# A mixture-of-experts stage on one Trainium2 core: 21 units of expert work instead of 22, two of them cut into strips of 64, 32 and 32 slots

## The reference, cut to what matters

```python
# h: 1024 tokens x 1024; N_GROUPS = 4, EXPERTS_PER_GROUP = 8, so 32 experts; EXPERT_FF = 512
gsel = argmax(h @ rg + rgb)                    # one group for each token
top_v, top_i = top_k((h @ re + reb)[gsel], 2)  # two experts in that group
wts = softmax(top_v) * p_group
# for each token and each of its two experts e:
y += wt * ((silu(h @ w1[e]) * (h @ w3[e])) @ w2[e])   # w1, w3: 1024x512, w2: 512x1024
x = rms_norm(x + y) * norm_final
```

## Time and profile before

| what | value |
| --- | --- |
| time, median of 3 runs | 2502.93 us (2500.17 to 2503.08) |
| profiled execution, its own time | 2497.98 us |
| span in its profile, first to last instruction | 2496.2 us |
| busy share of the span | PE 97%, PEld 52%, DVE 50%, ACT 23%, POOL 4% |
| mean granted clock of TensorE | 0.988 |
| HBM read, written | 329.07 MB, 68.26 MB |

### The profile page before, as it was taken

The page is one execution under the profiler, slowest core; times in us unless marked ns, Lnnn a source line. Parts: engine busy times, 40 slices in busy tenths (PEclk is TensorE's granted clock), DMA queues, the critical chain, the costliest instruction groups (busy, mean ns, idle before and its releaser), DMA issues. The chain is left out here.

```text
span 2496.2 us, 39012 instructions
## 1 busy us (share of the span) xinstructions
PE 2412.2 (97%) x16519; PEld 1288.4 (52%) x16519; DVE 1243.1 (50%) x2080; ACT 570.2 (23%) x949; POOL 99.8 (4%) x97
## 2 busy tenths in 40 slices
PE   9999999999999999989999999999999999999996
PEld 5644557454565454744445976644455444443342
DVE  4646676767675858563585634465444411101103
ACT  3322323223232424121111354411100000000002
POOL 1000000000000000000000000000000100000002
PEclk9999999999999999999999999999999999999998
DMA  4111212121212121122434823163263999999997
GB/s 155 40 49 38 70 49 70 45 70 49 70 45 64 38 79 35 61 65 73 161 76 127 302 97 102 39 208 109 74 220 133 413 428 428 427 427 424 428 428 294
DMA packets 214908, 406.18 MB, mean 163 GB/s; under 512 B 64979, under 2 KB 166861, under 8 KB 202445
## 3 DMA queue, kind: packets, MB, share of 16 engines
q1 hardware_dynamic: 187152, 336.42, 36.9%
q10 hardware_dynamic: 22108, 47.32, 5.2%
q0 software_dynamic: 5472, 19.93, 2.1%
HBM read 329.07 MB, written 68.26 MB: 159 GB/s over the span
## 5 line engine op out<-in xcount | busy, mean ns | idle before, releaser
L3317 PE MATMUL moe_pp<-moe_ring,own_xT 128*128 128x512 f32 (+1 forms) x624 | 235.5, 599 | 1.4 <-DVE own_xT L3072 1.4
L3175 DVE COPY own_hidT<-moe_pp 128x512 f32<-128x512 f32 x22 | 15.2, 691 | 270.9 <-PE moe_pp L3326 270.9
L3317 PEld LDWEIGHTS moe_pp<-moe_ring,own_xT 128*128 128x128 f32 (+1 forms) x624 | 89.7, 167 | 107.0 <-issue 105.0
L742 PE MATMUL rwkv_pp<-mix_hT,rwkv_side_raw 128*128 128x512 f32 x240 | 116.7, 621 | 8.0 <-DMA rwkv_side_raw<-w_in 4.1
L3340 PE MATMUL moe_pp<-moe_ring,own_hidT 128*64 128x512 f32 (+1 forms) x368 | 120.1, 594 | 0.8 <-DVE own_hidT L3175 0.8
L2881 PE MATMUL moe_pp<-moe_ring,mix_hT 128*128 128x512 f32 x256 | 117.5, 610 | 3.3 <-DVEq L179 3.3
L671 PE MATMUL rwkv_pp<-mix_hT,rwkv_wt_kv 128*128 128x512 f32 x256 | 113.3, 595 | 0.0
L742 PE MATMUL rwkv_pp<-rwkv_TS,rwkv_side_sum 128*128 128x512 f32 x240 | 109.9, 601 | 2.8 <-ACT rwkv_TT L1259 1.7
L742 PE MATMUL rwkv_pp<-rwkv_TS,rwkv_side_raw 128*128 128x512 f32 x240 | 110.6, 603 | 0.8
L1682 DVE TENSOR_TENSOR rwkv_Sf<-rwkv_pp,rwkv_LY 128x64 f32<-128x64 f32 x128 | 28.7, 225 | 161.0 <-PE rwkv_pp L1023 161.0
L2309 PE MATMUL attn_pp<-att_yC,attn_wp 128*128 128x512 f32 x224 | 100.7, 597 | 0.0
(11 more groups left out here) (493 smaller groups left out, 4459.3 us busy)
## 6 DMA issues: line engine op xcount, KB each, us to landing
moe_ring<-moe_w SPq DMA_DIRECT2D x54, 2048.0 KB, 31.6
mix_yAB<-moe_w SPq DMA_DIRECT2D x18, 2048.0 KB, 32.4
mix_hT<-moe_w SPq DMA_DIRECT2D x17, 2048.0 KB, 31.7
rwkv_side_raw<-w_in SPq DMA_DIRECT2D x20, 1024.0 KB, 5.4
s_y<-mix_yAB SPq DMA_DIRECT2D x24, 512.0 KB, 11.8
moe_ring<-moe_w ACTq DMA_DIRECT2D x6, 2048.0 KB, 9.0
s_y<-own_yo ACTq DMA_DIRECT2D x22, 512.0 KB, 10.4
rwkv_wt_kv<-w_in SPq DMA_DIRECT2D x16, 512.0 KB, 4.4
```

The lines of the kernel that those rows point to most:

```text
L742: mm = pe.matmul(pp[:, bank, :], left[:, part, :], right[:, part, :], start=fresh and part == 0, stop=part == HK - 1, skip_group_check=True)
L3175: dve.tensor_copy(hidT[:, :, :].rearrange("p k s -> p (k s)"), pp[:, 4, :]).then_inc(hidT_s, 1)
L3317: mm = pe.matmul(pp[at, bank, :], xT[n % 2][:, kt, at], weights(w, n, h)[0][:, kt, :], start=kt == 0, stop=kt == KT - 1)
```

## The change

The number of units falls from 22 to 21. The unit of rank 31 and rank 3's surplus is gone. Instead the two whole units with the fewest tokens, ranks 11 and 12 (`LENDERS = 2`), keep 96 slots and lend 32: rank 11 to the surplus of rank 3, rank 12 to rank 31. A function `columns` gives the strips of a unit for the matmuls: one of 128 in a whole unit, two of 64 in a shared one, and in the two lending units three: 64 and 32 columns with the lender's weights, 32 columns with the borrower's. The unit order changes from place 9 on: pairs of small experts are now two in a row at places 8 and 9, rank 3 and the unit (11, 3) stand at 10 and 11, and the list ends (29, 30), (12, 31), (10). The 96 weight loads stay 96, in the new order. `room` computes the new capacities and offsets, with 14 chained instructions on VectorE in place of 10. The ranges of the loops, the ring, the transfers of one unit and everything after the units are as before.

```diff
-WHOLE = 13
-SMALL = N_EXPERTS - WHOLE
-UNITS = WHOLE - STATIC_HALVES // 2 + (SMALL + 1) // 2
-TOP_HALF = 2 * UNITS - 1
+WHOLE = 13
+LAST = N_EXPERTS - 1
+HALVES = LAST - WHOLE
+LENDERS = 2
+UNITS = WHOLE - STATIC_HALVES // 2 + HALVES // 2
...
+    wholes = [((r,), r - shared) for r in range(TOP + 1, WHOLE - LENDERS)]
+    pairs = [((WHOLE + 2 * j, WHOLE + 2 * j + 1), WHOLE - shared + j) for j in range(HALVES // 2)]
+    pairs.append(((WHOLE - 1, LAST), WHOLE - 1 - shared))
+    top = [((TOP,), TOP - shared), ((WHOLE - 2, TOP), WHOLE - 2 - shared)]
...
+    middle = len(wholes) // 2
+    return first + mixed(pairs[:middle + 2], wholes[:middle]) + top + mixed(pairs[middle + 2:-1], wholes[middle:-1]) + [pairs[-1], wholes[-1]]
+
+def columns(ranks):
+    if len(ranks) == 1:
+        return [(0, slice(0, SLOTS))]
+    if WHOLE - LENDERS <= ranks[0] < WHOLE:
+        cut = SLOTS - QUARTER_SLOTS
+        return [(0, slice(0, HALF_SLOTS)), (0, slice(HALF_SLOTS, cut)), (1, slice(cut, SLOTS))]
+    return [(0, slice(0, HALF_SLOTS)), (1, slice(HALF_SLOTS, SLOTS))]
...
             def room():
                 link(dve.scalar_tensor_tensor(out=base[:, :], in0=rank[:, :], scalar=float(WHOLE), in1=rank[:, :], op0=ALU.min, op1=ALU.add))
-                link(dve.tensor_scalar(cap[:, :], rank[:, :], float(WHOLE), float(HALF_SLOTS), ALU.is_lt, ALU.mult))
-                link(dve.scalar_tensor_tensor(out=cap[:, :], in0=rank[:, :], scalar=float(STATIC_HALVES), in1=cap[:, :], op0=ALU.is_ge, op1=ALU.mult))
+                link(dve.tensor_scalar(cap[:, :], rank[:, :], float(STATIC_HALVES), -2.0, ALU.is_ge, ALU.mult))
+                for r in (WHOLE - LENDERS, WHOLE, LAST):
+                    link(dve.scalar_tensor_tensor(out=cap[:, :], in0=rank[:, :], scalar=float(r), in1=cap[:, :], op0=ALU.is_ge, op1=ALU.add))
...
             def up(w, bank, done, n):
                 landed(pe, w, n)
-                many = len(RANKS[n])
-                rows = P // many
                 for kt in range(KT):
-                    for h in range(many):
-                        at = slice(h * rows, h * rows + rows)
+                    for h, at in columns(RANKS[n]):
                         mm = pe.matmul(pp[at, bank, :], xT[n % 2][:, kt, at], weights(w, n, h)[0][:, kt, :],
                                        start=kt == 0, stop=kt == KT - 1)
                 mm.then_inc(done, 1)
```

More of the change, by code:

```diff
@@ L61 @@
 HALF_SLOTS = SLOTS // 2
+QUARTER_SLOTS = SLOTS // 4
 STATIC_EXPERTS = (0, 2, 1)
@@ L81, in unit_order, with mixed, lent @@
 def unit_order():
-    assert SMALL // 2 == WHOLE - TOP - 1
+    assert HALVES % 2 == 0
     shared = STATIC_HALVES // 2
[L86 to L92, removed]
-    first = [(tuple(range(STATIC_HALVES)), 0)] + [((r,), r - shared) for r in range(STATIC_HALVES, STATIC)]
-    return first + mixed(slice(0, middle)) + top + mixed(slice(middle, None))
+    wholes = [((r,), r - shared) for r in range(TOP + 1, WHOLE - LENDERS)]
+    pairs = [((WHOLE + 2 * j, WHOLE + 2 * j + 1), WHOLE - shared + j) for j in range(HALVES // 2)]
+    pairs.append(((WHOLE - 1, LAST), WHOLE - 1 - shared))
+    top = [((TOP,), TOP - shared), ((WHOLE - 2, TOP), WHOLE - 2 - shared)]
+    first = [(tuple(range(STATIC_HALVES)), 0)] + [((r,), r - shared) for r in range(STATIC_HALVES, STATIC)]
+    def mixed(twos, ones):
+        return [unit for two in zip(twos, ones) for unit in two] + twos[len(ones):]
+    middle = len(wholes) // 2
[7 more added lines that the diff above has]
+    return [(0, slice(0, HALF_SLOTS)), (1, slice(HALF_SLOTS, SLOTS))]
+def lent(i):
+    return (WHOLE - i - STATIC_HALVES // 2 + 1) * SLOTS - QUARTER_SLOTS
 RANKS, BLOCK_OF = zip(*unit_order())
@@ L3106, in room @@
                 link(dve.scalar_tensor_tensor(out=base[:, :], in0=rank[:, :], scalar=float(WHOLE), in1=rank[:, :], op0=ALU.min, op1=ALU.add))
-                link(dve.tensor_scalar(cap[:, :], rank[:, :], float(WHOLE), float(HALF_SLOTS), ALU.is_lt, ALU.mult))
-                link(dve.scalar_tensor_tensor(out=cap[:, :], in0=rank[:, :], scalar=float(STATIC_HALVES), in1=cap[:, :], op0=ALU.is_ge, op1=ALU.mult))
+                link(dve.tensor_scalar(cap[:, :], rank[:, :], float(STATIC_HALVES), -2.0, ALU.is_ge, ALU.mult))
+                for r in (WHOLE - LENDERS, WHOLE, LAST):
+                    link(dve.scalar_tensor_tensor(out=cap[:, :], in0=rank[:, :], scalar=float(r), in1=cap[:, :], op0=ALU.is_ge, op1=ALU.add))
                 link(dve.scalar_tensor_tensor(out=base[:, :], in0=base[:, :], scalar=-float(STATIC_HALVES), in1=rank[:, :], op0=ALU.add, op1=ALU.max))
                 link(dve.tensor_scalar(base[:, :], base[:, :], float(HALF_SLOTS), None, ALU.mult))
-                link(dve.tensor_scalar(cap[:, :], cap[:, :], float(HALF_SLOTS), None, ALU.add))
-                link(dve.tensor_scalar(shift[:, :], rank[:, :], float(TOP), float(HALF_SLOTS), ALU.is_equal, ALU.mult))
+                link(dve.tensor_scalar(exc[:, :], rank[:, :], float(LAST), float(lent(1) - (LAST + WHOLE - STATIC_HALVES) * HALF_SLOTS), ALU.is_ge, ALU.mult))
+                link(dve.tensor_tensor(base[:, :], base[:, :], exc[:, :], ALU.add))
+                link(dve.tensor_scalar(cap[:, :], cap[:, :], -float(QUARTER_SLOTS), float(HALF_SLOTS), ALU.mult, ALU.add))
+                link(dve.tensor_scalar(shift[:, :], rank[:, :], float(TOP), float(QUARTER_SLOTS), ALU.is_equal, ALU.mult))
                 link(dve.tensor_tensor(cap[:, :], cap[:, :], shift[:, :], ALU.add))
-                link(dve.tensor_scalar(shift[:, :], shift[:, :], float(TOP_HALF - 2 - 2 * TOP + STATIC_HALVES), None, ALU.mult))
+                link(dve.tensor_scalar(shift[:, :], shift[:, :], float(lent(2) - (TOP - STATIC_HALVES // 2 + 1) * SLOTS) / QUARTER_SLOTS, None, ALU.mult))
                 link(dve.tensor_tensor(exc[:, :], tot, cap[:, :], ALU.subtract))
```

## The result

The median of four runs is 2540.1 us (2537.59 to 2544.24), that of the kernel before, with one more run than above, 2502.41 us. The ratio is 1.0152, 95% interval 1.0138 to 1.0166: 37.7 us slower. The profiled execution of the changed kernel has a span of 2537.4 us, 41.2 more than before.

A forecast was written before the change was run, and what follows sets the result against it. TensorE was taken to set the end, with the DMA right behind it. One unit fewer (-22.3 us) and mixed strips (+54.3), all else nothing, gave +32.0 us: 2535 us, range 2522 to 2555.

The forecast's parts named there:

- What bounds the kernel: Expert stage: TensorE sets the end, the DMA is right behind it; 7.2 us of waiting for data.
- One unit fewer: TensorE: 22 units of 22.3 us become 21, -22.3 us; the 96 weight loads stay.
- Strips of 64, 32 and 32: Two lending units: each change of shape empties TensorE, a stage takes 16.1 us, not 7.02; six stages +54.3 us.
- the step of a lending unit: Sign in TensorE's timeline: the step of units (11, 3) and (12, 31) near 49 us instead of 22.3.
- The waits, kept as they were: TensorE's loss to late weight loads stays 7.2 us, from nothing (-7.2) to twice as much (+7.2).
- the 14 that would have made the term wrong: Sign: idle time for weight loads before L3317 and L3340 beyond 14 us would make the waits term wrong.
- the order of units: Two pairs in a row at places 8 and 9: DMA is ahead there, cost nothing; at most 15 us if late.
- VectorE's chain and what follows the last matmul: Four more instructions in `room`, hidden in idle time (0.9 us without cover), and the unchanged tail: nothing.
- The sum: Whole kernel: -22.3 + 54.3 + 0 = +32.0 us, 2534.9 for the median.
- The rival "faster": Lending units: three strips run side by side at no cost, DMA sets the end, -5.8 us, median 2497; chance 0.12.
- Partly side by side: Lending units: three strips share the room of two, a stage 10.5 us, about 2501 with waits; chance 0.09.
- record by record: Lending units: strips take turns by record, a place 2.29 us, a stage 18.3, +45.5 in all, 2548; chance 0.11.

## Why the prediction was right

The measured 2540 us lies in the range, 5 us above the forecast. Step by step:

- **What bounds the kernel.** Right on both sides. With its loads halved the stretch of the kernel before became 7.1 us shorter, against the 7.2 read from the chain. With a unit fewer and four strips of 32, TensorE had 20.9 us less to do and the stretch became only 3.8 us shorter.
- **One unit fewer, -22.3 us.** It was -20.9. The mean of a step was the wrong price: the change takes away two whole units of 22.0 us and one shared one of 22.55 and puts two units of the shared kind in their place, 66.6 - 45.1 = 21.5 us; 0.6 us stay unexplained.
- **Strips of 64, 32 and 32, +54.3 us.** The mechanism and the size were right: 53.1 us, 8.86 a stage against 9.05, 1.99 us a place against 2.01. The emptying of TensorE at a change of shape, seen in the kernel before only between 128 columns and fewer, holds between 64 and 32 as well, so the rule of the Trainium skill (page "TensorEngine Tiling (Array Packing)", section "Key Properties") stands for this change too; the trace now shows it at each place of the mixed stages. A slip beside it: the step of a lending unit was to be near 49 us. But from one `turn` to the next a step holds only two of the unit's three stages, since its `lower` comes behind the next unit's: for (11, 3) one step is 2229.43 - 2189.25 = 40.2 us, and the one after the next 31.3.
- **The waits, kept as they were.** This is the term that was too small: 12.6 us, not 7.2, inside the bound of twice as much; the idle time in it is 7.4 us, under the 14 that would have made the term wrong. 3.7 of the 5.5 us more come at the part that I costed at nothing, the order of units. Load 45, the last w2 of the pair at place 8, was issued at 2133.6 and landed 32.4 us later, at 2166.0, so TensorE stood for 1.92 us and then took 8.78 us for a stage instead of 7.02. The DMA was ahead at that point, as I wrote, but not by enough. In the kernel before, the last w2 of that pair is load 43. It was issued at 2123.7 us and landed 27.9 us later, at 2151.6, 8.8 us ahead of the stage that uses it (2160.42 in the chain). The change puts two more loads ahead of it, and load 45 of the kernel before landed at 2162.2, 10.6 us behind its load 43. The price that I gave as the worst for this part, 15 us, was not reached. Of the 3.7 us the part from the low clock, 8.78 - 7.02 = 1.8, need not have come: the kernel with the strips grouped by shape and the one with four strips stood still at the same place for 1.88 and 2.00 us, and their clock stayed at 1.00. The rest, 1.8 us, is at the two later waits (ended at 2346.18 and 2395.19 us in the chain): 5.5 us of standing still and 8.80 + 8.65 - 2 x 7.02 = 3.4 us from the low clock, 8.9 in all where before it was 7.1. Why these two grew wasn't looked into.
- **VectorE's chain and what follows the last matmul: nothing.** The stretch from the last matmul to the end is 46.3 us against 45.9, and the first `own_xT` is still released by TensorE's transposes, after 4.08 us idle.
- **The sum.** 32.0 - 1.2 for the strips + 1.4 for the unit + 5.5 for the waits = 37.7 us.
- **The rival "faster".** Its premise is false for this cut, but its sum could be tested with four strips of 32: -5.8 us were worked out, -3.8 measured in the stretch, 0.15% in the time. "Partly side by side" and "record by record" are out: a place is neither 1.3 nor 2.29 us.

## What to carry to other kernels

In these kernels (float32, weights 128x512) matmuls on separate strips of columns ran side by side only where neighbours had one shape; with a mix of 64 and 32 columns TensorE took turns, and the single wide strip then had the engine for itself. Where a stage needs mixed widths, try cutting everything in it to the narrowest one: here four strips of 32 cost 7.05 us, and 64 with 32 and 32 cost 15.88. And before counting what work saved on one engine is worth, ask how far behind the next resource is: here the loads were already late by 7 us, and of 20.9 us saved on TensorE 17.1 came back as waits.

## What the runs showed of the hardware that was not expected

- The four strips of 32 run at the full rate although four matmuls are under way at once (three of them with the same weight rows) and each record has a weight load record of its own: 0.43 us for four records, as for one of 128 columns. The experiment's theory had it so, but no row of the kernel before showed it.
- Behind an idle time of 1.92 us in the changed kernel the clock fell: the first 9 us have a granted clock of 0.81, with 32 records in 8.78 us. The first 2 us are near the lower level of 1.2 GHz, and from 2170 us on the clock is at 2.4 GHz again:

```profile
2166.00:2175.00 9.00, 8.94 (x33) 3.38 (x34) 0.00 (x0) 0.12 (x1) 0.00 (x0) 0.81 1.00 420
2166.00:2168.00 2.00, 1.94 (x6) 0.82 (x8) 0.00 (x0) 0.00 (x0) 0.00 (x0) 0.57 1.00 426
2170.00:2172.00 2.00, 2.00 (x12) 0.79 (x10) 0.00 (x0) 0.00 (x0) 0.00 (x0) 1.00 0.97 403
```

In the kernel with four strips of 32 a slightly longer pause at the same place of the code, behind the same work, was followed by the usual rate (its timeline), and so was one of 1.88 us in the kernel with the strips grouped by shape:

```profile
2163.92 7.09 PE L3356 MATMUL moe_pp<-moe_ring,own_hidT 128*64 128x512 f32 x32 [2.00 <-issue]
```

In the kernel before, 2.76 us of idle time behind the last unit were followed by 16 records in 7.13 us, the usual rate too:

```profile
2453.05 7.13 PE L3410 MATMUL moe_pp<-mix_hT,main_ident 128*128 128x512 f32 x16 [2.76 <-issue]
```

So neither the length of a pause nor the work ahead of it tells whether the clock falls; what else decides it was not tried. Of a late load, the standing still can be worked out from the rows, while the low clock behind it may come or not: here it was worth 1.76 us.
